# Even mixer's output product as three passes of halves, with half-wise residual signals and high halves first

## What is computed

```python
xn = rms_norm(x, norm_mix[0])
hcat = xn @ w_in                                  # 1024 -> 1952
out_a = neighbourhood_attention(q, k, v, rpb)     # 8 heads of 64
c_q, c_kv = rms_norm(hcat[.., q part], ..), rms_norm(hcat[.., kv part], ..)
out_b = dense_attention(q, k, v)                  # 8 latent heads of 64
x = x + concat([out_a, out_b]) @ w_o              # 1024 -> 1024: the even mixer's output product
x = x + square(relu(rms_norm(x) @ w1)) @ w2
x = x + odd_mixer(rms_norm(x, norm_mix[1]))
x = x + square(relu(rms_norm(x) @ w1')) @ w2'
return rms_norm(x)
```

## Time and profile before

| | |
|---|---|
| runs, median (lowest to highest) | 1237.68 us (1237.54 to 1241.94) |
| the profiled execution's own time | 1237.45 us |
| its span, first to last instruction | 1235.6 us |
| mean granted TensorE clock | 0.991 of 2.4 GHz |
| TensorE matmuls busy | 1179.7 us (95%) |
| VectorE, ScalarE, GpSimd busy | 748.7, 556.4, 51.7 us |
| moved by DMA | 209.73 MB, 170 GB/s |

### The profile page before, as it was taken

One profiled execution on the slowest core, in us unless ns is written; L12 is line 12 of the kernel. 1 busy time (PEld: TensorE's weight loads), 2 busy tenths in 40 slices (PEclk: granted clock), 3 DMA queues, 4 the chain that ended last, 5 costly groups with the idle time before them and its releaser, 6 DMA issues.

```text
span 1235.6 us, 18834 instructions
## 1 busy us (share of the span) xinstructions
PE 1179.7 (95%) x7401; PEld 1020.6 (83%) x7401; DVE 748.7 (61%) x991; ACT 556.4 (45%) x735; POOL 51.7 (4%) x60
## 2 busy tenths in 40 slices
PE   4899998999999989899999999999999999999997
PEld 1577785689999978647999998999999987999996
DVE  1579336374555566664565456777777878654653
ACT  3862242353433363553344245655555556433432
POOL 2000033000000060000000000000000000000000
PEclk9999999999999989999999999999999999999999
DMA  9683472899564560516555643555554424855410
GB/s 315 217 284 131 141 273 40 292 252 282 172 184 154 159 163 1 215 59 216 206 190 184 234 110 103 153 154 153 153 137 127 143 90 159 297 176 204 172 61 35
DMA packets 201056, 209.73 MB, mean 170 GB/s; under 512 B 5819, under 2 KB 166854, under 8 KB 200806
## 3 DMA queue, kind: packets, MB, share of 16 engines
q1 hardware_dynamic: 197536, 201.61, 51.8%
q0 software_dynamic: 1648, 5.03, 1.6%
q10 hardware_dynamic: 1814, 2.30, 0.6%
HBM read 207.86 MB, written 2.01 MB: 170 GB/s over the span
## 4 chain that ended last, share of the span: by engine, by line
PE 88%; DVE 7%; ACT 2%; DMA 2%; issue 1%; ACTq 0%; DVEq 0%
PE bank L1978 23%; PE bank L1979 22%; PE bank L1980 22%; PE bank L2232 2%; PE bank L1825 2%; PE bank L1826 2%; PE bank L1827 2%; PE bank L2361 1%; PE bank L2342 1%; PE bank L2351 1%; PE bank L1776 1%; DMA normed<-in_ctx_dram 1%; PE bank L2332 1%; DMA weight_pool<-in_mod_w_dram 1%; PE bank L1944 1%
## 5 line engine op out<-in xcount | busy, mean ns | idle before, releaser
L1978 PE MATMUL bank<-hT_high,mlp_up_high 128*128 128x256 f32 x512 | 145.2, 284 | 1.1 <-DVE hT_low L1422 1.1
L1979 PE MATMUL bank<-hT_low,mlp_up_high 128*128 128x256 f32 x512 | 144.9, 283 | 0.0
L1980 PE MATMUL bank<-hT_high,mlp_up_low 128*128 128x256 f32 x512 | 144.9, 283 | 0.0
L1978 PE MATMUL bank<-od_w_high,hT_high 128*128 128x384 f32 x384 | 132.7, 346 | 1.7 <-DVE hT_low L1422 1.4
L1980 PE MATMUL bank<-od_w_high,hT_low 128*128 128x384 f32 x384 | 128.7, 335 | 0.0
L1979 PE MATMUL bank<-od_w_low,hT_high 128*128 128x384 f32 x384 | 128.4, 334 | 0.0
L1111 DVE TENSOR_TENSOR mlp_down_low<-weight_pool,mlp_down_high 128x2048 fp32r<-128x2048 f32 x32 | 73.3, 2289 | 59.2 <-ACT mlp_down_high L643 59.2
L1978 PE MATMUL bank<-hT_high,ffn_up_high 128*128 128x256 f32 x352 | 99.7, 283 | 2.9 <-DVE hT_low L1111 2.9
L1978 PEld LDWEIGHTS bank<-hT_high,mlp_up_high 128*128 128x128 f32 x512 | 98.1, 192 | 2.9 <-issue 2.0
L1978 PE MATMUL bank<-mlp_down_high,hidden_high 128*128 128x512 f32 x256 | 99.9, 390 | 0.0
L1979 PE MATMUL bank<-mlp_down_low,hidden_high 128*128 128x512 f32 x256 | 99.9, 390 | 0.0
(11 more groups left out here) (331 smaller groups left out, 2672.9 us busy)
## 6 DMA issues: line engine op xcount, KB each, us to landing
weight_pool<-in_mlp_w_dram SPq DMA_DIRECT2D x64, 1024.0 KB, 7.6
weight_pool<-in_od_w_in_dram SPq DMA_DIRECT2D x72, 512.0 KB, 5.2
weight_pool<-in_mod_w_dram SPq DMA_DIRECT2D x22, 1024.0 KB, 10.9
weight_pool<-in_ffn_w_in_dram SPq DMA_DIRECT2D x44, 512.0 KB, 5.6
weight_pool<-in_gla_w_in_dram SPq DMA_DIRECT2D x12, 1024.0 KB, 6.8
weight_pool<-in_ffn_w_out_dram SPq DMA_DIRECT2D x22, 512.0 KB, 6.2
weight_pool<-in_gla_w_out_dram SPq DMA_DIRECT2D x2, 2048.0 KB, 14.3
weight_pool<-in_ev_w_in_dram SPq DMA_DIRECT2D x4, 1024.0 KB, 6.6
```

Of the source, the lines that this page charges most:

```text
L1978: mm(out_, left[0], right[0], start=start, stop=False, **flag)
L1979: mm(out_, left[0], right[1], start=False, stop=False, **flag)
L1980: return mm(out_, left[1], right[0], start=False, stop=stop, **flag)
```

## The change

The even mixer's output product is made of halves. ScalarE copies the high part of each pair's heads from PSUM in its loop, VectorE's copy of the heads becomes the low part and waits for the high one (`o_hi`). ScalarE writes the high parts of the eight weight row blocks (four at the end of rounds 4 to 7, one in round 8, three behind the loop); GpSimd writes the first four low parts, VectorE the other four behind its loop. TensorE's `ev_out` waits for the low parts and does three passes.

The residual signals `res_ready` after each half of a tile, the transposes wait for halves, and `y_half` is also given for the bank 2. The last step of each MLP and the last rows of the output products are ordered by bank. The gated update is two instructions of 512 columns. `c_product(0)` (now in bank 0) and the odd mixer's first `od_proj` do all products with high tokens first, and those with low tokens behind them. Semaphores `go_hi`, `go_lo`, `go_lo_dve` become `wo_hi`, `wo_lo`, `wo_lo_dve` and count on; `vn_act` becomes a count of `mv_out`.

```diff
@@ tensors
-        oT = view(hTs, 2048, KD, SEQ)
+        oT2 = [view(over(f"ev_heads_{w}", where, at, 2048), 0, KD, SEQ) for w, where, at in (("high", "hT", 2048), ("low", "normed", 0))]
+        EV_ROWS = (4, 5, 6, 7, 0, 1, 2, 3)
+        eoH = {k: over(f"ev_out{k}_high", where, at, D) for k, (where, at) in zip(EV_ROWS, EO_HIGH)}
+        eoL = [over(f"ev_out{k}_low", "weight_pool", 8192 + D * k, D) for k in range(KD)]
+        def y_ready(n, b):
+            return (s["y_half"], max(2 * n, 1)) if b < 2 else (s["y_half"], 2 * n + 1) if n and b == 2 else y_done(n)
@@ GpSimd, behind the bias
+            for i, k in enumerate(EV_ROWS[0:4]):
+                g.wait_ge(s["wo_hi"], KD + i + 1)
+                g.tensor_tensor(eoL[k][:, :], pool[...], eoH[k][:, :].bitcast(F32), ALU.subtract).then_inc(s["wo_lo"], 1)
@@ ScalarE
+            def ev_out_high(k):
+                high(eoH[k], e, D * (k % 4), e.value, "wo_hi")
+            def ev_heads_high(p):
+                act.wait_ge(s["pv_ps"], p + 1)
+                act.activation(oT2[0][:, (p + 4) % 8, :], bank[EV_OUT[p % 2]][:, 0:SEQ], ACT.Copy).then_inc(s["o_hi"], 1)
             for q in range(U_OD // 2 + 1):
                 for u in (2 * q, 2 * q + 1):
                     if q < U_OD // 2:
                         ev_exp(u)
+                    if u % 2 == 0 and q >= 3:
+                        ev_heads_high(q - 3)
                     if q:
                         ev_turned(u - 2)
+                    if u % 2 and 4 <= q < U_OD // 2 or u % 2 == 0 and q == U_OD // 2:
+                        ev_out_high(EV_ROWS[q - 4])
...
+            ev_heads_high(6)
+            ev_out_high(EV_ROWS[5])
+            ev_heads_high(7)
+            ev_out_high(EV_ROWS[6])
+            ev_out_high(EV_ROWS[7])
@@ VectorE
-                dve.scalar_tensor_tensor(out=res[:, t, :], in0=xn[:, t, :], scalar=stat[:, 86 + t:87 + t], in1=res[:, t, :],
-                                         op0=ALU.mult, op1=ALU.add).then_inc(s["res_ready"], 1)
+                for h in range(2):
+                    v = res[:, t, 512 * h:512 * h + 512]
+                    dve.scalar_tensor_tensor(out=v, in0=xn[:, t, 512 * h:512 * h + 512], scalar=stat[:, 86 + t:87 + t], in1=v,
+                                             op0=ALU.mult, op1=ALU.add).then_inc(s["res_ready"], 1)
...
             def ev_out(p):
-                dve.wait_ge(s["pv_ps"], p + 1)
-                dve.tensor_copy(oT[:, (p + 4) % 8, :], bank[EV_OUT[p % 2]][:, 0:SEQ]).then_inc(s["o_out"], 1)
+                dve.wait_ge(s["o_hi"], p + 1)
+                low(oT2[1][:, k, :], bank[EV_OUT[p % 2]][:, 0:SEQ], oT2[0][:, k, :], "o_out")
...
-            for p in (6, 7):
-                ev_out(p)
+            ev_out_low(4)
+            ev_out(6)
+            ev_out_low(5)
+            ev_out(7)
+            ev_out_low(6)
+            ev_out_low(7)
@@ update(n, t)
-                dve.wait_ge(*((s["y_half"], n + 1) if t == 0 else y_done(n)))
                 for h in range(2):
+                    dve.wait_ge(*y_ready(n, 2 * t + h))
...
-                ins.then_inc(s["res_ready"], 1)
+                    ins.then_inc(s["res_ready"], 1)
@@ TensorE
                 for t in range(NT):
-                    pe.wait_ge(s["res_ready"], 2 * (n - 2) + t + 1)
-                    for b in RAW_ORDER:
+                    for i, b in enumerate(RAW_ORDER):
+                        if i % 2 == 0:
+                            pe.wait_ge(s["res_ready"], 4 * (n - 2) + 2 * t + i // 2 + 1)
...
+            def high_first(out_, stage, low0, weights):
+                for n, k in enumerate(K_ORDER):
+                    if n % 2 == 0:
+                        pe.wait_ge(s["hT_hi"], RAW_HI[stage] + n // 2 + 1)
+                    for i, w in enumerate(weights(k)):
+                        mm(out_, hT2[0][:, k, 0:P], w, start=(n == 0 and i == 0), stop=False, skip_group_check=True)
+                for n, k in enumerate(K_ORDER):
+                    if n % 2 == 0:
+                        pe.wait_ge(s["hT_lo"], low0 + n // 2 + 1)
+                    ins = mm(out_, hT2[1][:, k, 0:P], weights(k)[0], start=False, stop=(n == KD - 1), skip_group_check=True)
...
                 for k in range(k0, k0 + kn):
-                    landed_wait(e)
+                    pe.wait_ge(*((s["wo_lo"], 6 + EV_ROWS.index(k) + 1) if k >= 4 else (s["wo_lo_dve"], 2 + EV_ROWS.index(k) - 3)))
                     pe.wait_ge(s["o_out"], (k + 4) % 8 + 1)
-                    for b in (2 * t, 2 * t + 1):
-                        ins = mm(bank[b][:, :], oT[:, k, P * t:P * t + P], pv(e)[:, k % 4, 512 * (b % 2):512 * (b % 2) + 512],
-                                 start=(k == 4), stop=(k == 3))
+                    for b in (2 * t + h for h in half):
+                        ins = split_mm(bank[b][:, :], both(oT2, lambda x: x[:, k, P * t:P * t + P]),
+                                       both((eoH[k], eoL[k]), lambda x: x[:, 512 * (b % 2):512 * (b % 2) + 512]), k == 4, k == 3)
...
-            ev_out(1, 0, 4).then_inc(s["out_used"], 1)
+            ev_out(1, 0, 4, (0,)).then_inc(s["y_half"], 1)
+            ev_out(1, 0, 4, (1,)).then_inc(s["out_used"], 1)
@@ last MLP step
-                        for f, b in ((0, 2 * t), (0, 2 * t + 1), (1, 2 * t), (1, 2 * t + 1)):
+                        parts = ((0, 2 * t), (0, 2 * t + 1), (1, 2 * t), (1, 2 * t + 1))
+                        for f, b in sorted(parts, key=lambda x: x[1]) if last else parts:
```

More of the change, by code:

```diff
@@ L601, in norm_stats @@
                 for t in range(NT):
-                    act.wait_ge(ready, count if n < 2 else count - 1 + t)
+                    act.wait_ge(ready, count if n < 2 else count - 2 + 2 * t)
                     at = NS + 6 * n + t
@@ L2246, in _ @@
                 if q == 2:
[L2247 removed]
+                    pe.wait_ge(s["mv_out"], 3)
                 if q >= 2:
```

112 lines of the change are left out of this document (63 added, 49 removed).

## The result

The changed kernel takes 1242.97 us (median of 18 runs, 1240.95 to 1243.88) against 1237.47 us before (18 runs, 1235.33 to 1242.24): a ratio of 1.0042, 95% interval 1.0034 to 1.0051, or 5.5 us more. The forecast was 1243.1 and "same within 0.5%". The profiled execution has a span of 1241.0 us for 1235.6.

The account below looks back on a forecast made before the run. TensorE, with 88% of the span, bounds the kernel, but not its attention loop. Loop and product +7.5, port +0.7, clock +2.5 and borders −5.3 sum to +5.4 us: 1243.1 us, own range 1240.5 to 1246.

Parts of the forecast that it names:

- The mechanism: Attention loop, from round 3: VectorE stops at the low heads until ScalarE's high heads, behind exp(2q), are ready; 2.4 us idle.
- The loop, +13.4: Even mixer's attention loop: round 3 costs 2.2 us, round 4 2.4, rounds 5 to 7 2.9 each; 7.4 us against 4.42.
- the last round adds none: End of the attention loop: no added time, since its low weights (1.22 us each) stand in waits for TensorE.
- the −1.5 of its pieces: Four output-product pieces between the attention's own instructions at the loop's end, on the path, save 1.5 us.
- The dense run, −4.4: Even mixer's output product behind the loop: twelve pieces, each 0.37 us shorter as single passes, save 4.4 us.
- The port, +0.7: Loop's end: GpSimd's fourth low weight can hold VectorE's last scaling; 0 to 1.4 us, middle taken.
- The clock, +2.5: Attention loop: TensorE's gaps may drop the clock to 1.2 GHz; 0 if it stays, 5 us if down throughout.
- the forecast's case: Attention loop: granted clock under 1, priced at +2.5 us, between staying up and being down throughout.
- the first rival: Clock down through loop and product's start: +7.7 us, 1245.4 us; chance 0.20.
- The borders, −5.3: Stage borders: half-wise residual updates and high halves first let TensorE start earlier; 5.3 us saved, 4.1 to 6.7.
- first border: Mixed output to feed-forward: gains nothing, as two modulation slices on TensorE cover the two halves' 0.1 us.
- The faster rival: Low heads, rounds 3 to 7: high heads do not hold VectorE; −10.2 us, 1227.5 us; chance 0.09.

Follow-up runs that it names:

- e4: Changed kernel with VectorE's low heads of pair q-3 put behind maximum and scale of unit 2q-1 instead of 2q-2: 1232.69 us, ratio 0.9947.
- e12: Changed kernel with ScalarE's high heads put one step later, behind the copy of turned probabilities of unit 2q-2: 1247.64 us, ratio 1.0075.
- e8: Changed kernel with three unread 256-column matmuls ahead of TensorE's turn of unit 2q-2 in rounds 3 to 7: 1248.27 us.
- e9: Changed kernel with three unread 256-column matmuls ahead of TensorE's turn of unit 2q-1 in rounds 3 to 7: 1240.18 us, ratio 1.0020.
- e10: e9 with GpSimd's four low weights cut to 8 columns and the high weights read in their place: 1239.37 us.
- e5: Changed kernel with GpSimd's four low weights cut to 8 columns and the high weights read in their place: 1243.25 us.
- e2: Kernel before with only the even mixer's output product made of halves, no border changed: 1248.43 us, ratio 1.0078.
- e1: Changed kernel with the even mixer's output product left as one fp32 product, so only the border changes remain: 1232.36 us, ratio 0.9956.
- e6: e4 with GpSimd's four low weights cut to 8 columns and the high weights read in their place: 1227.32 us, ratio 0.9922.
- e11: e4 with all low weights made on VectorE behind the loop; TensorE multiplies rows 4 to 7 by high weights first, low ones later: 1227.61 us, ratio 0.9912.

## Why the prediction was right, point by point

- **The mechanism** is as put: low heads with an idle time ahead of them that high heads end, in the rounds named (2.6 to 3.2 us, where the forecast had 2.4). e4 takes it away (−10.3), e12 lengthens it (+4.7), e8 lengthens it from TensorE's side (+5.3).
- **The loop, +13.4.** At the held clock of e9 the low heads of pair 4 come 12.2 us later after the first turn than the copy before did (542.43 − 505.59 = 36.84 for 533.26 − 508.66 = 24.60), where rounds 3 to 7 were to cost 13.4. A round is 7.08 us, not 7.4 (the pieces listed come to 7.5 if the 0.15 for hand-overs is added to the turn). ScalarE is the part that was charged too much: from the exp that waits to the low heads it takes 3.80 us (531.55 to 535.35), for 4.2 in the sum, since each of its instructions starts about 0.1 us before the one ahead of it ends. The step "the last round adds none" failed: the low heads of pair 5 come 6.09 us after those of pair 4 for 4.23 before, +1.9, and stood still for 2.90 us behind the exp, the copy and the weight copy of round 7. Against that the end of the loop gave back more than the −1.5 of its pieces: without port and at full clock (e10) 5.50 us for 8.33, −2.8. The three misses, −1.2, +1.9 and −1.3, nearly cancel, and that is luck.
- **The dense run, −4.4:** −4.2.
- **The port, +0.7 (0 to 1.4):** 1.35 on the path by e9 and e10, 1.3 by e5, so the upper end. My reason for the middle, that no scaling of before was seen next to GpSimd, was caution where the rows of another VectorE instruction already told it. By the rule that the Trainium skill gives (SBUF — State Buffer, Who interferes with whom) the scaling had to be caught; the trace agrees, 2.05 us for 0.62.
- **The clock, +2.5 (0 to 5):** 1.7 in the loop by the traces of e9 and the changed kernel, 2.8 by their medians. The traces of e2 and e5, with the same rounds, were 0.9 and 0.8 us slower there than the changed kernel's, so the price varies from run to run, from 1.7 to about 2.7. It fell for a part of the loop (0.80 and 0.87), not through it, which is the forecast's case and not the first rival's. That the low clock goes with TensorE's gaps, and not with VectorE's standstill as such, is borne out by e9 and e10: with the gap filled and the standstill still at 2.6 us, 516 to 533 and 533 to 546 are at 1.00 and 1.00, 1.00 and 0.87, where the three traces of the same rounds without filler have 0.80 and 0.87, 0.80 and 0.69 (e5), 0.80 and 0.68 (e2). e12, with longer gaps, has 0.72 and 0.76.
- **The borders, −5.3 (−4.1 to −6.7):** −4.7 in the changed kernel's trace, −5.6 in e1. One by one, forecast and trace: first border 0 and 0; feed-forward to even −1.4 and −1.1 (e1: −1.9); even to MLP −0.9 and −0.8; MLP to odd −1.7 and −1.9, of which 0.3 is lost again at the next weights' low half (its product starts at 770.41, that half ends at 770.35), as the working said; odd to MLP −0.6 and −0.6; the last −0.7 and −0.7.
- **The sum:** loop with pieces, port and clock +14.4 (forecast 15.1), dense run −4.2, borders −4.7: +5.5, forecast +5.4. The loop's terms were off by 0.6 to 1.9 us each, and the loop's first turn alone starts anywhere between 505.59 and 508.77 in the traces of one and the same code ahead of it. That the total came within 0.1 us is luck; that it lay in the range is not.
- **The faster rival** was priced at 1227.5 with "high heads do not hold VectorE". e4, which is only that, gives 1232.7; it takes a free port as well to come there (e6 1227.3, e11 1227.6). The rival's own sum kept 1.0 us for all that the loop would still cost, and the port alone costs 5.4 (e4 against e6) when VectorE never stands still. Its condition, that ScalarE's 1.3 us of spare time nearly hold 1.5 more, was right: 4.67 us a round for 4.42.

What stays open: why the clock at the border from feed-forward to even mixer differs between runs of one and the same code (0.50 to 1.00 in 442 to 446, below). It decides whether that border gives 1.1 or 1.9 us.

## What to carry to other kernels

When work is handed from one engine to a second and back inside a software pipeline, write out both queues and look for what stands ahead of the new hand-over: here a copy of 0.36 us cost 2.0 to 2.7 us a round since it stood behind an exp that waited, through TensorE, for the very engine that waited for the copy. Move the consumer to the place in its queue where the producer is already done (one line here, 10 us), and then read the trace again, because a standstill hides what would collide with it: a port, a clock, a queue. A product's low parts need not be ready with its high parts; passes that use them can come last.

## What the runs showed of the hardware that I had not expected

- A `tensor_scalar` of VectorE from SBUF to SBUF (128x256, two of them 0.62 us) that begins beside a `tensor_tensor` of GpSimd waits for the end of that one instruction: 2.05, 2.11, 2.37 and 2.65 us. (The first of the two ends 0.15 us after GpSimd's, at 554.57 for 554.42 in the changed kernel.) Instructions of VectorE that read PSUM and SBUF were not held: in the changed kernel the low heads at 539.08 (0.42 us) and the scaled score with its bias at 539.42 (0.68 us) run at their usual length beside GpSimd's low weight from 537.76 to 540.11. Four instructions of 256 columns instead of one of 1024 let VectorE in between and brought the scalings to 1.09 to 1.65 us.
- The granted clock differs between runs where the code is the same. At the border from feed-forward to even mixer (442 to 446) it was 0.50 in the changed kernel and 1.00 in e10, whose instructions up to there are the same, and this has a price: over the 10 us from the feed-forward's last matmul, five traces with this border's code have a mean clock of 0.69 to 0.72 and take 69.9 to 70.1 us to the first turned probabilities, and seven have 0.83 to 1.00 and take 68.6 to 69.2. One profile can't price an edit there. The row of e10:

```profile
442.00:446.00 4.00, 2.76 (x16) 2.31 (x17) 3.10 (x8) 2.44 (x7) 4.00 (x7) 1.00 0.87 194
```

- A gap in TensorE's work that is filled with matmuls nobody reads can make a kernel faster (by 2.8 us in the medians) when it lies off the ring, and costs more than that (5.3 us) when it lies on it.
